# Prompt-output norm ahead of the sample attention, and the last out projection's prompt tiles between its pages

## The reference, cut to what matters

```python
def b_layer(h, ...):
    q, mem_q, gate = split(rms_norm(h, norm_g) @ w_in)
    o = attend(rope(rms_norm(q, q_g)), lam)             # prompt: causal; sample: 1024 past keys in 8 pages + 8 new
    o = rms_norm(o, subln_g) * (1 - lam_init)
    mo = mem_attend(mem_q, mem_k, mem_v, mq_g)
    y = concatenate([o, mo]) * silu(gate)
    return h + y @ w_out                                # y_prompt (1024, 1024), y_sample (64, 1024)
```

## Time and profile before

| | us |
|---|---|
| median of 3 runs | 2410.2 |
| the profiled execution's own time | 2412.64 |
| its span, first to last instruction | 2411.0 |
| TensorE busy | 2178.6 (90%) |
| VectorE busy | 907.3 (38%) |
| ScalarE busy | 635.4 (26%) |
| mean granted TensorE clock | 0.953 |

### The profile page before, as it was taken

One profiled execution on the slowest core, in us unless ns is written; L12 is line 12 of the kernel. 1 busy time (PEld: TensorE's weight loads), 2 busy tenths in 40 slices (PEclk: granted clock), 3 DMA queues, 4 the chain that ended last, 5 costly groups with the idle time before them and its releaser, 6 DMA issues. The chain is left out here.

```text
span 2411.0 us, 47179 instructions
## 1 busy us (share of the span) xinstructions
PE 2178.6 (90%) x20794; PEld 1412.5 (59%) x20794; DVE 907.3 (38%) x1765; ACT 635.4 (26%) x1433; POOL 317.1 (13%) x288
## 2 busy tenths in 40 slices
PE   6999999999999999989986999968898887898399
PEld 4576585775856758554643555545566555677243
DVE  4153452534625436232232303250322776343500
ACT  5222222322222232132222112131221665222100
POOL 0000020110201102020002112001000565121000
PEclk9999999999999999999988999989997999889599
DMA  6000010000100000016012112000002000796301
GB/s 247 29 19 11 10 40 18 29 20 10 39 18 28 21 10 30 20 61 225 1 48 79 54 54 108 1 0 35 27 27 71 1 1 13 285 314 230 144 35 39
DMA packets 51775, 147.84 MB, mean 61 GB/s; under 512 B 11331, under 2 KB 20867, under 8 KB 50036
## 3 DMA queue, kind: packets, MB, share of 16 engines
q1 hardware_dynamic: 40356, 99.51, 11.8%
q0 software_dynamic: 11216, 45.33, 5.2%
HBM read 123.58 MB, written 21.24 MB: 60 GB/s over the span
## 5 line engine op out<-in xcount | busy, mean ns | idle before, releaser
L755 PE MATMUL psum<-xT,rw_w 128*128 128x384 f32 (+1 forms) x1152 | 420.0, 493 | 2.8 <-PEq L169 2.8
L2046 PE MATMUL psum<-kvq_w,xT 128*128 128x384 f32 (+1 forms) x864 | 282.9, 490 | 13.2 <-POOL kvq_w L2000 13.2
L755 PEld LDWEIGHTS psum<-xT,rw_w 128*128 128x128 f32 x1152 | 200.4, 190 | 107.3 <-issue 10.9
L2046 PEld LDWEIGHTS psum<-kvq_w,xT 128*128 128x128 f32 (+1 forms) x864 | 159.1, 185 | 135.4 <-issue 22.5
L1286 DVE COPY rwkv_sa_sb<-psum 128x64 f32<-128x64 f32 x96 | 21.6, 225 | 264.9 <-PE psum L963 264.9
L1951 PE MATMUL psum<-xT,yT 128*128 128x512 f32 (+1 forms) x216 | 98.6, 607 | 13.9 <-DMA xT<-in_w_out 13.9
L1097 ACT COPY rwkv_r_sb<-psum 128x64 f32<-128x64 f32 x96 | 20.4, 213 | 339.0 <-PE psum L948 307.5
L723 POOL DMA_DIRECT2D out<-rwkv_s x6 | 5.7, 942 | 774.0 <-ACT rwkv_out_p L1118 774.0
L2112 DVE TENSOR_REDUCE kvq_ss<-kvq_sq 128x6 f32<-128x384 f32 (+1 forms) x36 | 19.9, 552 | 217.6 <-ACT kvq_sq L2084 217.4
L1461 PE MATMUL psum<-xT,y_r 128*128 128x512 f32 (+1 forms) x180 | 88.7, 626 | 7.6 <-DMA y_r<-gated 7.6
L1529 PE MATMUL psum<-xT,gate_w 128*128 128x384 f32 (+1 forms) x288 | 93.0, 473 | 1.9 <-POOL gate_w L1518 1.9
(11 more groups left out here) (427 smaller groups left out, 3851.6 us busy)
## 6 DMA issues: line engine op xcount, KB each, us to landing
xT<-in_cache_k SPq DMA_DIRECT2D x64, 384.0 KB, 6.4
samp_vp<-in_cache_v POOLq DMA_DIRECT2D x64, 384.0 KB, 5.1
rw_w<-in_w_in SPq DMA_DIRECT2D x28, 512.0 KB, 3.9
kvq_w<-in_kv_w SPq DMA_DIRECT2D x4, 1536.0 KB, 6.5
front_w<-in_mem_w_kv SPq DMA_DIRECT2D x2, 2048.0 KB, 14.3
x_rows<-in_x_p SPq DMA_DIRECT2D x8, 512.0 KB, 13.9
h<-in_x_p SPq DMA_DIRECT2D x8, 512.0 KB, 13.1
residual<-h POOLq DMA_DIRECT2D x8, 512.0 KB, 2.9
```

The lines of the kernel that those rows point to most:

```text
L755: mm = pe.matmul(out, w[:, load % 2, k, :], xT[:, k, a:b], start=(k == 0), stop=(k == KC - 1))
L2046: mm = pe.matmul(bank[0:r, j % 6, 0:W], xT[:, k, n * P:n * P + r], w[:, i % 2, k, :], start=(k == 0), stop=(k == KC - 1))
```

## The change

The prompt outputs' stage is moved ahead of the sample attention. While it runs, SyncE loads what the out projection needs: eight slices of the weights, 512 KB each, into six dead tiles of V and two of KT, and the first three residual tiles into KT. The out projection's stage is gone. Its eight prompt tiles are 16 units (tile and half) of 8 matmuls; these 128 matmuls are shared out evenly, two behind each page of the sample attention, with unit sums in banks 3 and 7 by turns. VectorE adds the residual where a unit ends (every fourth page). SyncE loads the other residual tiles and issues the stores, between its page loads. The ninth tile (64 sample rows) is computed at the end, its two halves in two halves of the partitions.

```diff
-def out_project(nc, name, w_d, yT, h, bank, scratch, h_load, h_store):
...
-def prompt_outputs(nc, QT, subs, gates, ident, bank):
+def prompt_outputs(nc, QT, subs, gates, ident, bank, ahead):
...
+        @block.sync
+        def _(sp):
+            for dst, src in ahead:
+                sp.dma_start(dst, src).then_inc(ahead_loaded, 16)
+            sp.wait_ge(ahead_loaded, 16 * len(ahead))
...
+class PromptSums:
...
+        self.units = [(n, half) for n in range(NT) for half in range(2)]
+        self.parts = [(u, k) for u in range(len(self.units)) for k in range(KC)]
+        count = B * PAGES
+        cuts = [g * len(self.parts) // count for g in range(count + 1)]
+        self.share = [range(cuts[g], cuts[g + 1]) for g in range(count)]
...
+    def page(self, sp, g):
+        if g % 8 == 2 and self.early + g // 8 < NT:
+            self.load(sp, self.early + g // 8)
+        if g == 60:
+            self.load_last(sp)
+        if g % 8 == 7 and g >= 15:
+            self.store(sp, (g - 15) // 8)
...
+    def pe(self, pe, g):
+        for x in self.share[g]:
...
+            if k == 0 and u >= 2:
+                pe.wait_ge(self.added, u - 1)
+            mm = pe.matmul(self.out(u), self.ys[k][:, n * P:(n + 1) * P], self.w[k][:, half * 512:(half + 1) * 512],
+                           start=(k == 0), stop=(k == KC - 1))
...
+    def dve(self, dve, g):
...
+                dve.wait_ge(self.unit_mm, u + 1)
+                if n >= self.early:
+                    dve.wait_ge(self.h_loaded[n], 16)
+                hh = self.h[n][:, half * 512:(half + 1) * 512]
+                self.nc.vector.tensor_tensor(hh, hh, self.out(u), ALU.add).then_inc(self.added, 1)
...
+    def pe_last(self, pe, y_ready):
+        pe.wait_ge(self.added, len(self.units))
+        for k in list(range(DH, KC)) + list(range(DH)):
+            if k == 0:
+                pe.wait_ge(y_ready, 1)
+            for half in range(2):
+                mm = pe.matmul(self.bank[half * NS:(half + 1) * NS, 3 + 4 * half, :], self.ys[k][:, SEQ:TT],
+                               self.w[k][:, half * 512:(half + 1) * 512], start=(k == DH), stop=(k == DH - 1))
...
@@ sample_attention, tensor @@
                     turn(2 * g + 1)
                     if pg:
                         scores(g - 1)
+                    between.pe(pe, g)
...
             mm.then_inc(o_turned, 1)
+            between.pe_last(pe, y_ready)
@@ sample_attention, vector @@
                     nc.vector.tensor_copy(kT[:, g % 2, 1, :], bank[:, 5, 0:H3 * P]).then_inc(dve_out, 1)
+                    between.dve(dve, g)
                 if b + 1 < B:
                     fill_queries(b + 1)
...
+            dve.sem_inc(y_ready, 1)
+            between.dve_last(dve)
@@ build @@
-        sample_attention(nc, i["pages"], i["cache_k"], i["cache_v"], KT, QT, V, lam, subs, yT, const, ident, bank, wide, xT, mq)
-        prompt_outputs(nc, QT, subs, yT, ident, bank)
...
-        out_project(nc, "out1", i["w_out"][1], y, h_rows, bank, xT, h_tiles, (y_p, y_s))
...
+        w_rows = [dead_v[:, k * D:(k + 1) * D] for k in range(6)] + [KT[:, k, 0:D] for k in (3, 4)]
+        h_rows = [KT[:, n, 0:D] for n in range(3)] + [QT[:, n, 0:D] for n in range(5)]
+        prompt_outputs(nc, QT, subs, yT, ident, bank,
+                       ahead=[(w_rows[k], i["w_out"][1][:, k * D:(k + 1) * D]) for k in range(KC)] +
+                       [(h_rows[n], h_tiles[0][n * P:(n + 1) * P, :]) for n in range(3)])
+        sums = PromptSums(nc, w_rows, y, h_rows, QT[:, DH - 1, 0:512], h_tiles, (y_p, y_s), 3, bank)
+        sample_attention(nc, i["pages"], i["cache_k"], i["cache_v"], KT, QT, V, lam, subs, yT, const, ident, bank, wide, xT, mq, sums)
```

More of the change, by code:

```diff
@@ L149 @@
 STORES = ("front_shift_stored front_kv_stored rwkv_stored rwkv_y_stored out0_stored kvq_k_stored kvq_v_stored "
-          "out1_stored").split()
+          "samp_stored").split()
 class Stage:
@@ L2339, in prompt_outputs @@
         ss = st.sb("ss", [P, DH * NT])
-        sq_ready, ss_ready, rs_ready, on_ready, turned, y_ready, dve_chain, act_chain = st.sems(
-            "sq_ready ss_ready rs_ready on_ready turned y_ready dve_chain act_chain")
+        sq_ready, ss_ready, rs_ready, on_ready, turned, y_ready, ahead_loaded, dve_chain, act_chain = st.sems(
+            "sq_ready ss_ready rs_ready on_ready turned y_ready ahead_loaded dve_chain act_chain")
         block = st.block()
+        @block.sync
[3 more added lines that the diff above has]
+            sp.wait_ge(ahead_loaded, 16 * len(ahead))
         def o(h):
@@ L2392, in _, with __init__, begin, out @@
                 mm.then_inc(turned, 1)
-def sample_attention(nc, pages_d, cache_k, cache_v, KT, QT, V, lam, subs, gates, const, ident, bank, wide, scratch, spare):
+class PromptSums:
+    def __init__(self, nc, w, ys, h, h_last, h_load, h_store, early, bank):
+        self.nc, self.w, self.ys, self.h, self.h_last, self.h_load, self.h_store, self.early, self.bank = (
+            nc, w, ys, h, h_last, h_load, h_store, early, bank)
+        self.units = [(n, half) for n in range(NT) for half in range(2)]
[3 more added lines that the diff above has]
+        self.share = [range(cuts[g], cuts[g + 1]) for g in range(count)]
+    def begin(self, st):
+        self.h_loaded = {n: st.sem(f"h_loaded{n}") for n in range(self.early, NTILE)}
+        self.unit_mm, self.added, self.last_mm, self.last_added, self.stored = st.sems("unit_mm added last_mm last_added stored")
+    def out(self, u):
+        return self.bank[:, 3 + 4 * (u % 2), :]
+    def load(self, sp, n):
+        sp.dma_start(self.h[n], self.h_load[0][n * P:(n + 1) * P, :]).then_inc(self.h_loaded[n], 16)
+    def load_last(self, sp):
+        for half in range(2):
+            sp.dma_start(self.h_last[half * NS:(half + 1) * NS, :], self.h_load[1][:, half * 512:(half + 1) * 512]).then_inc(
+                self.h_loaded[NT], 16)
+    def store(self, sp, n):
+        sp.wait_ge(self.added, 2 * n + 2)
+        sp.dma_start(self.h_store[0][n * P:(n + 1) * P, :], self.h[n]).then_inc(self.stored, 16)
+    def page(self, sp, g):
[5 more added lines that the diff above has]
+            self.store(sp, (g - 15) // 8)
+    def finish(self, sp):
+        for n in range((B * PAGES - 1 - 15) // 8 + 1, NT):
+            self.store(sp, n)
+        sp.wait_ge(self.last_added, 1)
+        for half in range(2):
+            sp.dma_start(self.h_store[1][:, half * 512:(half + 1) * 512], self.h_last[half * NS:(half + 1) * NS, :]).then_inc(self.stored, 16)
+        sp.wait_ge(self.stored, 16 * (NT + 2))
+    def pe(self, pe, g):
+        for x in self.share[g]:
+            u, k = self.parts[x]
+            n, half = self.units[u]
+            if k == 0 and u >= 2:
+                pe.wait_ge(self.added, u - 1)
+            mm = pe.matmul(self.out(u), self.ys[k][:, n * P:(n + 1) * P], self.w[k][:, half * 512:(half + 1) * 512],
+                           start=(k == 0), stop=(k == KC - 1))
+            if k == KC - 1:
+                mm.then_inc(self.unit_mm, 1)
+    def dve(self, dve, g):
+        for x in self.share[g]:
+            u, k = self.parts[x]
+            if k == KC - 1:
+                n, half = self.units[u]
+                dve.wait_ge(self.unit_mm, u + 1)
[8 more added lines that the diff above has]
+                pe.wait_ge(y_ready, 1)
+            for half in range(2):
+                mm = pe.matmul(self.bank[half * NS:(half + 1) * NS, 3 + 4 * half, :], self.ys[k][:, SEQ:TT],
+                               self.w[k][:, half * 512:(half + 1) * 512], start=(k == DH), stop=(k == DH - 1))
+        mm.then_inc(self.last_mm, 1)
+    def dve_last(self, dve):
+        dve.wait_ge(self.last_mm, 1)
+        dve.wait_ge(self.h_loaded[NT], 32)
+        for half in range(2):
+            hh = self.h_last[half * NS:(half + 1) * NS, :]
+            ins = self.nc.vector.tensor_tensor(hh, hh, self.bank[half * NS:(half + 1) * NS, 3 + 4 * half, :], ALU.add)
+        ins.then_inc(self.last_added, 1)
@@ L2401, in sample_attention @@
+def sample_attention(nc, pages_d, cache_k, cache_v, KT, QT, V, lam, subs, gates, const, ident, bank, wide, scratch, spare, between):
     R = DH * 2 * TS
@@ L2430, in sample_attention @@
         (pages_loaded, q_ready, turned, act_out, dve_out, k_used, s_mm, mx_ready, exp_ready, join_ready, w_mm, w_ready, o_mm,
-         sq_ready, ss_ready, rs_ready, o_ready, o_turned, v_used, dve_chain, act_chain) = st.sems(
+         sq_ready, ss_ready, rs_ready, o_ready, o_turned, y_ready, v_used, dve_chain, act_chain) = st.sems(
             "pages_loaded q_ready turned act_out dve_out k_used s_mm mx_ready exp_ready join_ready w_mm w_ready o_mm "
-            "sq_ready ss_ready rs_ready o_ready o_turned v_used dve_chain act_chain")
+            "sq_ready ss_ready rs_ready o_ready o_turned y_ready v_used dve_chain act_chain")
+        between.begin(st)
         block = st.block()
@@ L2448, in _ @@
```

(4 more changed lines are left out.)

2 lines of the change are left out of this document (1 added, 1 removed).

## The result

| | before | changed |
|---|---|---|
| median, us | 2411.89 (4 runs) | 2391.74 (4 runs) |
| lowest and highest | 2408.53, 2415.01 | 2387.74, 2395.24 |
| ratio of the times, 95% interval | | 0.9918, 0.9896 to 0.994 |
| profiled execution, own time and span | 2412.64, 2411.0 | 2394.83, 2392.7 |

The change makes the kernel 20 us faster (0.8%); 2384 us was forecast, with a range of 2370 to 2400.

What follows compares the result with a forecast made beforehand. TensorE was taken to bound the sample attention. Moved matmuls and other terms sum to 308.6 us against 334.4 us for the two stages replaced, 25.8 us fewer: 2384 us forecast, range 2370 to 2400.

Steps and rivals of the forecast that it cites:

- The sum from the start of the sample attention: Sample attention's first act to the span's end: 308.6 us, against 334.4 us for the two stages replaced.
- The step that carries the forecast: Sample attention: TensorE has no idle time for the 128 moved matmuls, so they cost their full time, 13.67 us per sequence.
- A sequence at full clock: One sample-attention sequence with its 16 moved matmuls: 32.0 us, where 18.68 us stood before; 256.0 us for eight.
- the switches: Each page's further change between kinds of matmul: 2 us taken over 64 pages, at most 7.7 us, at least nothing.
- the wait for `joined`: TensorE's wait behind a sequence's values: grows by 0.3 us, bounds 0 and 0.77; as a sign, 0.6 to 1.4 us.
- Half clock: At the seven later sequence borders TensorE's clock falls: 1.8 us lost each, together 12.6 us, bounds 0 and 24.5.
- The end: After the last values: norm 6.4 us, ninth tile 9.8, two adds 1.5, then 4.8 from add to end.
- 22 to 24 us from the last values to the end: Sign at the kernel's end: last values to span's end takes 22 to 24 us, 22.5 by the terms.
- Late key pages (E): Rival: residual loads and stores in SyncE's queue delay key pages, 0.4 us on each of 64, giving 2410 us; 4%.
- Half clock throughout (D): Rival: clock does not recover between borders, so parts run at half clock; slower, all records so make 2490 us; 4%.
- Less left (C): Rival: half clock costs 3.5 us at every border, ninth tile partly without overlap: 2396 to 2402 us; 14%.
- More given back (B): Rival: denser work keeps the clock up at most borders, no switch price, full ninth-tile overlap: about 2371 us; 18%.

## Why the prediction was right

The sum from the start of the sample attention was 308.6 us; the profile has 311.2. In the one profiled execution 4.9 us more come from a later start of the changed stages (2048.70 against 2043.79), which the second profiled execution shows to be chance, and 0.5 from what lies outside the span; that makes the 8.0 us between 2386.8 and 2394.83. The 2.6 us are what is left of larger errors that partly cancel, which is luck: the eight sequences took 3.4 us more than the sum had and the last values 0.9, the end 1.7 less.

*The step that carries the forecast* was "the 128 moved matmuls find no idle TensorE to hide in. They are paid in full". The run with all of them in one piece shows it: the same time. Changing the two stages round gives nothing, so the gain is not in the order. It is the removed stage: the load of 12.0 us, which the prompt outputs cover (their length is unchanged), the ninth tile's overlap, the start and end of a stage, and one norm that now runs straight into the last tile. As an estimate from the rows: 12.4 us for the issue and the load (2266.20 to 2278.63), 4.7 for the ninth tile (13.7 to 9.0), 2.4 from the last transposes to the next stage, 0.8 at the end and 3.0 for the cold start make 23.3, where 23.2 were measured. The load and the overlap have a run that bears on each; how the rest is shared out is argued, not shown.

*The terms.* A sequence at full clock was 32.0 plus 0.25 for the switches. The run with the add moved gives 31.85 without the add; with its 0.81 us that is 32.66 (32.67 by the one sequence of the changed kernel without a fall), so 0.4 too little was set. Most of it is the wait for `joined`, which I let grow by 0.3 us and which grew by 0.63 (0.58 to 1.21). I took it that the values cover most of the chain to `joined`; they cover none of the add, which shows at its full length. The switch is 3.136 us for a page (five from 2130.31) less 3.079 (1.373 for one without parts, in the kernel before from 2141.15 to 2146.64, and four records of 0.4266): 0.057 us a page, 3.6 us over all and not 2. Half clock: 34.51 us (mean of six sequences, 2123.41 to 2330.49) less 32.66 is 1.85 us a border, where 1.8 was set. Only the mean was right: single borders cost nothing, 1.6 to 1.7 or 3.1 to 3.2 us in this execution, and 4.3 at the first and 1.6 to 1.7 at the six others in the second. The first sequence took 0.9 us more than set, the stretch to the last values 0.9 more (7.7, with a late value page of 0.7). The end was overpriced: ninth tile 9.0 for 9.8 (it overlaps by 1.97 and not 1.76; the half clock cost 1.9 of the 2 us set), adds 1.4 for 1.5, store 4.0 for 4.8. So "22 to 24 us from the last values to the end" failed: 20.8. The end with two stores of 128 KB on SyncE's queue is 0.8 us shorter than that with one of 256 KB on GpSimd's; no run separates the queue from the size. The Trainium skill (DMA: Bandwidth & Descriptors, Latency and other measured facts) has 0.4 us between the first bytes of the two, and the trace agrees in sign.

*The signs.* Sequences stand 33.4 to 36.2 us apart (32 to 35 was said, and three of them lie above, the first among them), key waits are 1.0 us, the wait for `joined` 1.2, no add is waited for by TensorE, the clock's mean is 0.93, the prompt outputs last 32.85 us, and in the one piece records take 0.427 us.

*The rivals.* Late key pages (E): no, 1.0 us in all. Half clock throughout (D): no, 1.00 between borders. (In its price a record at half clock is 0.84 - 0.427 = 0.41 us dearer, not 0.43; so the gain would be gone from some 63 records on, not 61.) Less left (C): the loss was 1.85 and not 3.5 us a border, though three of the seven came near C's price. More given back (B): not by itself, since six of seven borders still fell. But its mechanism is the right one to build on: put four parts in the thin stretch, and the clock falls at no border. "The thin stretch at a border is not shortened, it grows" was the reason against it, and the two versions with parts at the border show that this was the place.

*Open:* why the clock falls at one border and not at the next, with the same work at both (in the changed kernel and with the add moved), is not settled, and between two executions of the changed kernel the borders differ; nor is the smallest number of parts that keeps it up, since only 4 and 16 were run at the middle borders.

## What to carry to other kernels

Where one engine is the bound, as here, moving its work beside other work of the same engine gives nothing: what this change gained is the load, the borders and the serial last tile of the stage that went. Before spreading filler evenly, list the waits and put the filler in front of those: the change with its 128 matmuls spread over pages gave 22 us, with some of them in front of the waits 56 (medians of 2392.21 and 2358.43 against 2413.99 us beside them). And look at what queues behind the filler's own small step on the next engine: an add of 0.69 us in the wrong place cost some 10 us of the sample attention by the traces (8 by the medians), half of it through the clock.

## What the runs showed of the hardware

- Two groups of 64 columns with 512-column matmuls overlap to a factor of 1.97 at full clock (24 records in 5.32 against 10.46 us); with six parts ahead of it the whole tile runs at full clock and takes 7.1 us (2342.79 to 2349.88), where 32 records of 0.427 us one behind the other are 13.7.
- One fall of the clock at a border costs 1.7 us of a sequence of 31.85 with the add moved; in the changed kernel 1.6 to 4.3 us, beyond one of 32.67. Two executions of the changed kernel fell at six and at seven of the seven borders and took 240.8 and 240.4 us over the same stretch.
- With 4 of a sequence's 16 matmuls at the border the granted clock stood at 1.00 from the second sequence's start to the last weights (2115 to 2330 us): sequences of 31.38 us, six times the same to 0.01 us. With all 16 there it stood at 1.00 as well (2124 to 2313).
